# Block 1's value and output products among the gather steps of a hybrid decoder trunk

## The reference

```python
def layer_ab(h, w_in, w_alpha2, b_alpha2, gla_norm, w_out):
    p = h @ w_in
    q_sb, k_sb, v_sb, q_g, k_g, v_g, g_g, a_lr = jnp.split(p, AB_SPLITS, axis=-1)
    o_sb = stick_breaking(heads(q_sb, SB_HEADS), heads(k_sb, SB_HEADS), heads(v_sb, SB_HEADS))
    ...
    mix = jnp.concatenate([o_sb, o_g], axis=-1).astype(h.dtype)
    return mix @ w_out

def peer(h, w_q, subkeys, u_tab, v_tab):
    q = (hf @ w_q).astype(jnp.float32).reshape(t_, PEER_HEADS, 2, PEER_QHALF)
    scores = jnp.einsum('thpd,hpnd->thpn', q, subkeys.astype(jnp.float32))
    # top 16 of each half, top 16 of their sums: idx, gate
    u_sel = u_tab[ii]
    act = jax.nn.gelu(jnp.einsum('td,tkd->tk', xi, u_sel).astype(jnp.float32), approximate=False)
    w = (gi * act).astype(v_tab.dtype)
    return jnp.einsum('tk,tkd->td', w, v_tab[ii])

for i in range(DEPTH):
    h = rmsnorm(x, norm_mix[i])
    x = x + (layer_ab(h, ...) if i % 2 == 0 else layer_c(h, ...))
    x = x + peer(rmsnorm(x, norm_ffn[i]), peer_w_q[i], ...)
return rmsnorm(x, final_norm)
```

## Time and profile before

| | us |
|---|---|
| median of 3 runs | 1602.76 |
| lowest, highest | 1600.73, 1605.67 |
| the profiled execution | 1604.98 |
| its span | 1603.3 |
| TensorE busy | 1428.0 (89%) |
| VectorE busy | 978.4 (61%) |
| ScalarE busy | 667.4 (42%) |
| POOL busy | 656.9 (41%) |
| moved by DMA | 624.48 MB |

### The profile page before, as it was taken

The page is one execution under the profiler, slowest core; times in us unless marked ns, Lnnn a source line. Parts: engine busy times, 40 slices in busy tenths (PEclk is TensorE's granted clock), DMA queues, the critical chain, the costliest instruction groups (busy, mean ns, idle before and its releaser), DMA issues.

```text
span 1603.3 us, 14828 instructions
## 1 busy us (share of the span) xinstructions
PE 1428.0 (89%) x4442; PEld 703.6 (44%) x4442; DVE 978.4 (61%) x2484; ACT 667.4 (42%) x1853; POOL 656.9 (41%) x535
## 2 busy tenths in 40 slices
PE   7999999899967899899988899999989889797776
PEld 6656545465412334343353445345435345242222
DVE  1217576758747767553446756566556677777744
ACT  1514445444515345242334534344344454444433
POOL 1002443545523343353435533323344544556673
PEclk9999999999979999999999999999999999999999
DMA  7324999999999999999999999999999999999996
GB/s 289 131 108 179 383 422 421 421 421 421 421 422 421 421 421 414 421 422 421 421 406 414 408 400 421 422 420 401 423 421 414 422 420 407 421 421 421 421 421 274
DMA packets 86368, 624.48 MB, mean 390 GB/s; under 512 B 9728, under 2 KB 9872, under 8 KB 10640
## 3 DMA queue, kind: packets, MB, share of 16 engines
q0 software_dynamic: 73728, 536.90, 81.1%
q1 hardware_dynamic: 12384, 86.35, 13.3%
q10 hardware_dynamic: 176, 0.28, 0.0%
HBM read 622.45 MB, written 1.05 MB: 389 GB/s over the span
## 4 chain that ended last, share of the span: by engine, by line
PE 42%; DMA 35%; DVE 10%; ACT 5%; issue 4%; POOL 3%; SPq 0%; POOLq 0%; DVEq 0%; ACTq 0%
DMA ring<-in_peer_uv,experts 34%; PE acc L1636 23%; DVE ring L1292 5%; PE work L1416 5%; PE work L1399 4%; POOL ring L719 3%; PE work L1388 3%; PE acc L1599 1%; PE acc L1430 1%; ACT diag L923 1%; ACT gelus L921 1%; PE work L1443 1%; PE work L1492 1%; ACT L920 1%; ACT gelus L920 1%
## 5 line engine op out<-in xcount | busy, mean ns | idle before, releaser
L1636 PE MATMUL acc<-ring,diag 128*128 128x512 f32 x2048 | 975.4, 610 | 156.3 <-ACT diag L923 154.9
L719 POOL DMA_INDIRECT ring<-in_peer_uv,experts x512 | 647.4, 1264 | 840.7 <-PE acc L1636 697.3
L1292 DVE CUSTOM_DVE_ANT_0 ring<-ring,h 128x1024 f32<-128x1024 f32 x512 | 624.7, 1225 | 449.7 <-DMA ring<-in_peer_uv,experts 441.5
L1636 PEld LDWEIGHTS acc<-ring,diag 128*128 128x128 f32 x2048 | 366.7, 191 | 684.9 <-ACT diag L923 351.9
L920 ACT ACTIVATE gelus<-dots 128x1 f32<-128x1 f32 x512 | 103.2, 202 | 674.9 <-DVE dots L1292 674.0
L923 ACT ACTIVATE diag<-ident,gelus 128x128 f32<-128x128 f32 x512 | 205.5, 401 | 16.7
L921 ACT ACTIVATE gelus<-gelus,gates 128x1 f32<-128x1 f32 x512 | 150.8, 295 | 16.6
L1399 PE MATMUL work<-weights,hT 128*128 128x512 f32 x176 | 82.5, 597 | 0.0
L1416 PEld LDWEIGHTS work<-hT,weights 128*128 128x128 f32 x448 | 54.2, 192 | 6.2 <-issue 6.2
L1416 PE MATMUL work<-hT,weights 128*128 128x128 f32 x448 | 56.5, 275 | 0.0
L1399 PEld LDWEIGHTS work<-weights,hT 128*128 128x128 f32 x176 | 33.7, 193 | 41.3 <-issue 41.2
(11 more groups left out here) (250 smaller groups left out, 975.3 us busy)
## 6 DMA issues: line engine op xcount, KB each, us to landing
weights<-in_c_w_in SPq DMA_DIRECT2D x15, 1024.0 KB, 10.5
weights<-in_ab_w_in SPq DMA_DIRECT2D x8, 1024.0 KB, 7.6
ring<-in_peer_uv,experts POOLq DMA_INDIRECT x512, 14.8
weights<-in_peer_w_q SPq DMA_DIRECT2D x8, 1024.0 KB, 9.6
mixT<-in_c_w_in SPq DMA_DIRECT2D x6, 1024.0 KB, 9.2
more<-in_c_w_in SPq DMA_DIRECT2D x6, 1024.0 KB, 9.5
weights<-in_c_w_out SPq DMA_DIRECT2D x6, 1024.0 KB, 9.6
more<-in_peer_w_q SPq DMA_DIRECT2D x5, 1024.0 KB, 9.1
```

Of the source, the lines that this page charges most:

```text
L719: pool.indirect_dma_start(ring[:, t % SLOTS, :], None, uv_rows, bass.IndirectOffsetOnAxis(ap=experts[:, b, step:step + 1], axis=0))\
L1292: nc.vector.tensor_tensor_reduce(out=ring[:, k, 0:D], in0=ring[:, k, 0:D], in1=h[:, b, :], scale=1.0, scalar=0.0, op0=ALU.mult, op1=ALU.ad ...
L1636: last = nc.tensor.matmul(acc[2 * b + n][:, :], diag[:, k, :], ring[:, k, D + n * CH:D + (n + 1) * CH], start=False, stop=True, skip_group ...
```

## The change

- PROJV 1 leaves the prefix. It is now four pieces of two matmuls behind steps 13, 15, 17 and 19 of the first gather (PROJV, VMORE; function `late_values`), and its copy VTAKE is behind step 20.
- In the prefix `prob1` overwrites `scores1` and later scores overwrite a part of `scores`, so five of the eight 256 KiB pieces of these weights are loaded anew: four by SP behind the first score product (QDOT 0 0 0 (0,)), into `mixT` and `queries`, and one behind the second, into `queries`. The other three still lie in `scores`. Three of the five go to `mixT` in runs of 512 bytes.
- STICKE 2 to 5, KV and GLAREAD come right behind the logarithms, ahead of the second head's ranking; of that, parts 4 and 5 go behind steps 1 and 3. Its score rows move to slots 6 and 7 of `diag`.
- SOUT is behind step 21 (before: 0), OUT at 24, 26, 28, 30 and 43, 46, 48, 51 (before: 3, 14, 16, 18 and 20, 22, 24, 27), SPATIAL at 23 (6), CAUSAL at 37 (20), OADD at 53 (29), block 1's HTAKE at 60 (36).
- Block 1's query projections stand at 72, 85, 97 and 109, in the order m = 0, 1, 2, 3 (before: m = 1 at 40, 2 at 57, 0 at 77, 3 at 92); those of block 0 for m = 2 and 3 at 34 and 62 (before 31 and 69). QDOT 0 1 3, and with it QKEYS 1, moves from step 106 to step 120.

```diff
+PIECES_OF = {"VMORE": 1, "QMORE": 4, "ZMORE": 2, "OMORE": 2}
...
 def parts_of_layer0():
-    out = [(0, ("SOUT", 1)), (1, ("STAKE", 1)), (1, ("GLASTAT", 1)), (2, ("GLAMEAN", 1)), (3, ("GLAOUT", 1)),
-           (4, ("GLAT", 1)), (5, ("GLATAKE", 1)), (6, ("SPATIAL",)), (20, ("CAUSAL",))]
+    out = [(1, ("TOPK", *SECOND[:2], 1, 4)), (2, ("GLASTAT", 1)), (3, ("TOPK", *SECOND[:2], 1, 5)), (3, ("GLAMEAN", 1)), (4, ("GLAOUT", 1)),
+           (6, ("GLAT", 1)), (7, ("GLATAKE", 1)), (13, ("PROJV", 1)), (15, ("VMORE", 1, 1)), (17, ("VMORE", 1, 2)),
+           (19, ("VMORE", 1, 3)), (20, ("VTAKE", 1)), (21, ("SOUT", 1)), (22, ("STAKE", 1)), (23, ("SPATIAL",)), (37, ("CAUSAL",))]
...
-        + [("QTAKE", *SECOND), ("SOFTLN", 2, 3, 4, 5), ("GV", 1), ("QDOT", *SECOND), ("DTAKE", *SECOND), ("LOG", 2, 3, 4, 5), ("PROJV", 1)]
+        + [("QTAKE", *SECOND), ("SOFTLN", 2, 3, 4, 5), ("GV", 1), ("QDOT", *SECOND), ("DTAKE", *SECOND), ("LOG", 2, 3, 4, 5), ("STICKE", 2), ("STICKE", 3), ("KV", 1), ("STICKE", 4), ("STICKE", 5), ("GLAREAD", 1)]
         + ranked_now(0, 0, 1)[:5]
-        + [("STICKE", 2), ("STICKE", 3), ("KV", 1), ("TOPK", 0, 0, 1, 4), ("STICKE", 4), ("STICKE", 5), ("TOPK", 0, 0, 1, 5),
-           ("GLAREAD", 1)]
...
+        late_v = [mixT[:, 0:4, 0:P], mixT[:, 4:8, 0:P], mixT[:, 0:4, P:T], queries[:, 0, :], v_chunk[1][:, 0, :], queries[:, 1, :],
+                  v_chunk[1][:, 2, :], v_chunk[1][:, 3, :]]
...
+                elif kind == "QDOT" and args[:3] == [0, 0, 0]:
+                    sp.wait_ge(out_full, 2)
+                    sp.wait_ge(*filled(bank))
+                    for k in (0, 1, 2, 3) if args[3] == (0,) else (5,):
...
+                        sp.dma_start(late_v[k], src).then_inc(late_v_in, 16)
...
+            def late_values(n, b, q=0):
+
+                w = work[n % WB] if q else claim_bank(pe, n)
+                pe.wait_ge(late_v_in, 16 * 5)
+                for k in (2 * q, 2 * q + 1):
+                    last = nc.tensor.matmul(w[:, :], hT[:, k, b * P:(b + 1) * P], late_v[k], start=(k == 0), stop=(k == KT - 1))
+                if q == 3:
+                    last.then_inc(full[n % WB], 1)
```

More of the change, by code:

```diff
@@ L470, in trunk @@
         za, t1, la, bc = (keysT[:, 4 * k:4 * k + 4, :].rearrange("p a n -> p (a n)") for k in range(4))
-        early_scores = [diag[:, 2 * hd:2 * hd + 2, :].rearrange("p a n -> p (a n)") for hd in range(2)]
+        early_scores = [diag[:, 6 * hd:6 * hd + 2, :].rearrange("p a n -> p (a n)") for hd in range(2)]
         eb, enb, edec = (z[:, k * CH:(k + 1) * CH] for k in range(3))
@@ L511, in trunk @@
         v_chunk_in = [sem(f"v_chunk_in{k}") for k in range(2)]
+        late_v_in = sem("late_v_in")
         log_ready = sem("log_ready")
@@ L608, in _ @@
                         sp.dma_start(v_chunk[half], ab_w_in[2][:, 4 * half:4 * half + 4, :]).then_inc(v_chunk_in[half], 16)
+                elif kind == "QDOT" and args[:3] == [0, 0, 0]:
+                    sp.wait_ge(out_full, 2)
+                    sp.wait_ge(*filled(bank))
+                    for k in (0, 1, 2, 3) if args[3] == (0,) else (5,):
+                        src = ab_w_in[2][:, k, :]
+                        if k < 3:
+                            src = src.rearrange("p (a t) -> p a t", t=P)
+                        sp.dma_start(late_v[k], src).then_inc(late_v_in, 16)
                 elif kind == "GQ":
@@ L827, in _ @@
                     stick_prob(args[0])
-                elif kind == "PROJV":
+                elif (kind == "PROJV" and args[0] == 0) or kind == "VTAKE":
                     w = await_bank(act, bank)
@@ L1553, in _ @@
                         wide(bank + 2 * k, await_chunk(pe, chunk + k), slice(0, T))
-                elif kind == "PROJV":
+                elif kind == "PROJV" and args[0] == 0:
                     values(bank, args[0])
+                elif kind in ("PROJV", "VMORE"):
+                    late_values(bank, *args)
                 elif kind == "STICKZ":
```

17 lines of the change are left out of this document (8 added, 9 removed).

## The result

| | before | after |
|---|---|---|
| median of 16 runs each, us | 1603.34 | 1606.41 |
| lowest, highest | 1600.73, 1605.67 | 1603.09, 1609.26 |
| span of the profiled execution | 1603.3 | 1606.9 |
| moved by DMA, MB | 624.48 | 625.79 |

The change made the kernel slower by 3.1 us: ratio 1.0022, 95% interval 1.0016 to 1.0028. That is inside 0.3%, and 1606.41 lies just under the upper end of the range, but on the other side of no change than the forecast of 2.6 us faster.

A forecast was written before the change was run, and what follows sets the result against it. The prediction took the DMA stream of gathered rows as the bound. Its terms, -4.7 + 0.6 + 1.2 + 0.3 = -2.6 us, took the median from 1602.76 to 1600.2 us, range 1596.0 to 1606.5.

The forecast's parts named there:

- (1): Prefix: block 1's value product leaves, so the suffix sums start earlier and row 6 is issued at about 149.4, not 155.96.
- (2): VectorE at the start: masks and state carry ahead of the second head's ranking; first row 2.8 us earlier, step 0 at 158.0.
- (3): Added DMA work, five 256 KiB pieces: four cost nothing in ten microseconds without traffic, the fifth costs 0.6 us.
- (4): First gather's queue: 4.7 us of idle DMA between 150 and 200 us goes; holes near rows 22 to 30 cost 1.2.
- (5): Output product and next query weights, steps 30 to 51: TensorE stalls 5 us, mostly hidden; cost 0.3 us, range to 2.
- (6): Later query parts, CAUSAL, spatial load, and layer-1 keys and weights loaded behind step 120 instead of 106: no cost.
- hidden, but barely: TensorE's 5 us stall at step 34: queued work lasts until about 261, row 43 is due at 262 to 263.
- estimate by the round-robin rule: Query weight loads at step 30: engines alternate between queue rows, so loads in after 10 us and the stall 3 us.
- no gain, thin queue: Rows 22 to 59 each wait on TensorE, so the 4.7 us come back: 1602 to 1604; chance 0.13.
- the clock at the start: TensorE idles from about 153.6 to 158.0; four first steps at 1.2 GHz would cost 7.7 us of TensorE.
- Slower, the load burst: Burst ends where the z projection begins, TensorE still at 1.2 GHz from step 135: 1607 to 1610; chance 0.11.
- More than that: The earlier start also closes later dips, at 620 to 630 and 830 to 850: -5.6 us, 1597.2; chance 0.22.

The follow-up runs named there:

- late weights, on the kernel before: Kernel before, with the last quarter of the output product's first half moved from step 18 to 27 and the second half's from 27 to 28; ratio 1.0000.

## Why the prediction was wrong, step by step

| step | forecast | measured |
|---|---|---|
| (1) row 6 issued | 149.4 | 148.7 |
| (2) first row on VectorE, step 0 on TensorE | 155.7, 158.0 | 154.8, 157.1 |
| (3) the loads | 0.6 | within 1.4 of nothing |
| (4) 150 to 200 us | -4.7 | -4.8 |
| (4) rows 14, 22, 30 issued | 175.3, 197.6, 218.6 | 174.9, 197.1, 222.7 |
| (4) holes at rows 22 to 30 | +1.2 | +1.7 |
| (5) weights asked for, in | 238.5, 250.4 | 242.6, 256.6 |
| (5) stand of TensorE | 5 | 7.18 |
| (5) second half's landing after the request | 11.9 | 14.0 |
| (5) row 43 issued | about 254 (data at 262 to 263, less 8.4) | 263.7 |
| (5) cost | +0.3 | +4.7 |
| (6) keys, z projection | 468, nothing | 478.3, nothing |

Steps (1) and (2) and the larger part of the fourth came out within 1 us; (3) can't be told from nothing. **The step that failed is the path from row 22 to row 30, and through it term (5).** For steps 15 to 22 the sum added TensorE's work alone: eight steps, three value pieces, the attention output. It left out ScalarE's queue between the last value piece and step 21: copy, two table loads, exponential, and only then GELU, gate and diagonal, 4.4 us in a row, of which TensorE sees 2.77, and the step behind it at half clock, 1.6 more (3.52 us for four passes instead of 1.88). The sum had that very mechanism for step 4, where it counted the two table loads of the GLA norm, and did not ask for it again where the change puts a copy that waits for TensorE ahead of another such pair. With both rows 30 is 4.1 us late, and by the same 4 us the weights are asked for late.

Term (5) then said "hidden, but barely". By its own numbers the queued work ends at 261 and a full stream would have row 43 in 2.49 us later, at 263.5; with row 43 due at 262 to 263 the margin is 0.5 to 1.5 us. Three inputs ate it:
- 4.1 us: the weights are asked for late, by the step-21 wait and the slow step behind it.
- 2.1 us: the load is in 14.0 us after the request, not 11.9. That is a misreading and not a slower load: 11.9 is the median over first and second halves, 9.6 to 14.3 in before, and the piece needs the second.
- 2.8 us: the clock behind the stand, which the sum left out: the piece 3.75 instead of 1.95, and 3.6 us from the start of step 35 to the issue of row 43 instead of 2.7.

Taking away the first, and with it 1.1 us of the third, brings the hole from 4.9 to 0.4. That this is close to the 0.3 of the sum is in part luck: in that run row 43 still went out 118.6 us after the first row, where the forecast has 114, and no hole came of it, because the stream too was later than in the sum. In the changed kernel row 42 is taken at 264.6, where the sum has it in at 261, so the real limit for row 43 was about 258.7 and not some 255. The mechanism of the term and its price for a late row were right; its inputs were too early. Its range, 0 to 2, was too narrow for a term that hung on a margin of about 1 us at the end of a chain of ten added durations.

The estimate by the round-robin rule that the prediction weighed (the Trainium skill, DMA: Bandwidth & Descriptors, section Queues, rings and completion order) would have had the load in after 10 us; the trace shows the first half in after 9.0 and the second 14.0 after the request, so for the half that counts it is further off than 11.9.

The rivals: *no gain, thin queue* is the nearest in kind: the queue was short, its 4.7 us came back and more, and rates under 400 stand between 200 and 300 us as it asked. It gave 1602 to 1604, and the time went 2.4 us beyond. But it had each of rows 22 to 59 late; it was one stand, and a smaller loss behind step 21. Its second cause, the clock at the start, is there (0.81 and 0.85) and costs nothing, as the run with the full clock shows. *Slower, the load burst*: the number nearly fits (1607 to 1610), the mechanism is refuted. The keys load at 478.29, the clock is low in the burst, and both recover ahead of the z projection, which begins at 538.11 with the DMA full throughout:

```profile
520.00:530.00 10.00, 7.62 (x11) 2.44 (x10) 5.83 (x15) 3.52 (x9) 1.88 (x2) 0.59 1.02 422
530.00:540.00 10.00, 7.37 (x23) 3.41 (x22) 8.85 (x24) 3.46 (x12) 3.25 (x3) 1.00 1.01 420
```

*More than that*: the dips behind did not close. The one at 620 to 630 (397) stands at 630 to 640 now, with the same 397, in a kernel that is some 3 us late; 830 to 840 reads 397 instead of 385, and 840 to 850 the same 360. From 600 to 1400 us the sum rose by 1.7. Whether that has to do with the change isn't settled: the same sum lies between 8.7 and 10.3 among the versions that are alike there.

## What to carry to other kernels

When work moves between the steps of a pipeline, add up not one engine but every in-order queue that the step passes: here a copy that waits for TensorE stood ahead of two table loads, made TensorE 4.4 us late (1.5 us of missing DMA time there), and the rest was paid 40 us later at another wait. When a load comes in halves and its user needs both, its time is that of the last half, not the median of the halves. Where a sum finds a stall "hidden, but barely", the term isn't worth its mean: its range must reach to the whole stall that appears when the inputs ahead of it are late. And of such a stall it is the date that counts at which the next row goes out, against the last queued row's arrival: using the weights later and taking lateness away ahead of it each gave back 5 us, while keeping the clock up in the stand gave 3.5. Asking for the weights earlier, and moving the exponential instead of the copy, weren't tried.

## What the hardware showed

- **The granted clock can fall at short stands, and half speed is paid by what comes next.** TensorE stands 4.29 us ahead of step 0 and the next six passes take 5.49 us:

```profile
157.07 5.49 PE L1657 MATMUL acc<-ring,diag 128*128 128x512 f32 x6 [4.29 <-ACT diag L933]
```

 The same behind 2.77 us (3.52 for four passes) and 7.18 us (3.75 for a query piece). In two versions the step behind the same 2.77 us ran at full speed (1.98), so the stand alone doesn't fix it. Unused multiplications in the stand kept the clock at 1.00 in the three versions that had them; at the start this gained nothing, in the late stand 2.3 us of row 43.
- **Two 1 MiB halves of weights, asked for 0.4 us apart on a full DMA, land well apart**: the first 9.0 us after its issue, the second 13.6 (9.6 and 14.3 in before). From the first request to TensorE's first use it took 14.0 to 14.7 us in the four versions in which TensorE stood for them at step 34. Where two more halves followed 3.4 us behind the first two (late weights, on the kernel before), those took 16.3 and 20.9.
- **A stand of 6.4 us with only eight rows of 2.49 us in the queue can cost 0.4 us**, and one of 7.2 us 4.9: in the first kernel the next row went out 6.2 us ahead of the arrival of the last queued one, in the second 0.9.
